# Hybrid decoder step on one core: mLSTM gate rows among the RWKV sample steps, output product evicted by ScalarE, gating ahead of the norm, other piece counts

## The chip, the cores and the metric

One NeuronCore of a Trainium2 chip runs the whole program. The metric is the time of one execution in microseconds (us) on the device. TensorE (PE) multiplies, VectorE (DVE) and ScalarE (ACT) work on elements, SyncE (SP) issues the weight transfers. GpSimd does nothing that matters here.

## The reference, cut to what matters

Two layers, for 256 prompt tokens and 8 sample tokens that share the weights. Only the parts that the change touches are shown.

```python
p = x @ lp['w_in']                                   # D_MODEL 2048 -> 6412 columns
p_rw, p_ret, p_ml = _split(p, [RW_P, RET_P, ML_P])
# RWKV-7: a state per head; the 8 samples take one step from their own state
s = exp(lw_t) * s - (kk_t * a_t) * sa + k_t * v_t    # sa = kk_t . s ; y = r_t . s
o_rw = (groupnorm(y) * g + b + bonus) * gate
# mLSTM: gates of 6 heads, one row of 264 tokens each
ig = CAP * tanh((im + ib) / CAP)
lf = log_sigmoid(CAP * tanh((fm + fb) / CAP))
b = cumsum(lf)                                       # per chunk of 128
m_i = max(running max of (ig - b), m of the chunk before)
s = (q . k) * exp(b_i - b_j + ig_j - m_i);  num = s @ v + ...;  den = sum(s) + ...
hid = num / max(|den|, exp(-m_i))
o_ml = sigmoid(om) * (_rmsnorm_heads(hid) * ml_norm)
# output product, residual, norm, feed-forward
mix = concatenate([o_rw, o_ret, o_ml]) @ lp['w_out']  # 2048 x 2048
x1 = _layernorm(ALPHA * x + mix, ...)
```

## The kernel before

Every large product runs on TensorE in three passes with operands split into a high and a low part. A slab is two blocks of 128 weight rows by 512 columns (512 KB). SP loads it into one of four `w_raw` places, ACT makes `w_hi` (L1202 between the mixers, L1189 in the loops), DVE makes `w_lo` (L1559, L1555), and both have a ring of four places too. So slab s+4 can't be split by ACT before TensorE is through with slab s.

A tile is one weight block of 128x128 for all tokens, that is three matmuls (L672 to L674). A slab holds 8 tiles, two for each of PSUM banks 0 to 3; banks 4 to 7 belong to the mixers. A group is 8 slabs in the input product, and 5 slabs (40 tiles) in the part of the output product that runs among the mLSTM steps. When a group closes, its four banks must be emptied; the next group's first tile in each bank waits on `bank_free` for that (`slab_tiles`, L676). The input groups are emptied by ACT inside `behind` (L1229 for the mLSTM columns), the output groups by DVE in `out_part` (L1574 adds the residual on the way, L1577 adds its low part).

The three mixers are chains of small steps on PE, ACT and DVE. They run one after the other, each beside a stream of tiles: retention beside five input groups, RWKV beside the last six, mLSTM beside 160 tiles of the output product. The steps have names, and a table (`ret_steps`, `rw_last`, `ml_steps`) says how many tiles PE runs ahead of each. `Behind.to(name)` on PE runs tiles up to that count. On ACT and DVE `Parts.to(name)` does the splitting and emptying that belong to those tiles, up to a slab that it works out from the same table, and only then the step's own instructions follow. Each engine has one queue, in the order in which the code is written:

```python
self.goals[name] = max(at_(before), at_(n) - 2, at_(max(n - 1, 0)) // slabs * slabs)
```

By this rule and the table the RWKV step `sa` stands at tile 240 of 368 in layer 0 and at tile 301 in layer 1. Tile 240 is the first of a group, tile 304 is the first of the next. ACT's goal at `sa` is slab 30 (layer 0) and 37 (layer 1), at `sv` it is slab 32 and 40; the emptying of the groups' banks goes with the last slab of a group, 31 and 39. In DVE `then` stands for an instruction, a wait for it, and one more slab's work where the goal of the step that follows leaves room.

The mLSTM part begins with the gate rows: DVE copies two sets of 6 rows (L2138 to L2140), ACT takes tanh, sigmoid and log (L1488 to L1491), DVE scans them and makes maxima (L2146 to L2170), ACT takes exponentials. PE then spreads rows over partitions with 6-row matmuls (`spread_m` L1129, `spread_e` L1138), and the attention steps follow: transposes (L802, L804), scores, numerators (`num0`, `num1`, L827 to L843), sample states (`vt`, `v0` to `v2`, `sy`), and the norm (`sumsq`, `spread` L886, `spread1` L891). The output's last step is the difference `o_lo` (L1867, `a_done`). PE's L1144 and the rest of the output product (`kblock`, L662 to L664) wait for it.

## Time and profile before

| | us |
|---|---|
| median of 3 runs | 2994.88 (2988.88 to 3004.73) |
| profiled execution | 3003.31 |
| its span | 3001.5 |
| PE busy | 2867.8 (96%) |
| PE weight load busy | 2746.3 (91%) |
| DVE busy | 1622.4 (54%) |
| ACT busy | 1171.5 (39%) |

The mean granted TensorE clock of the profiled execution is 0.959 of full speed. TensorE is busy nearly all the time, so its idle time and the stretches at the lower clock are what a reordering can touch. What each wait is for matters more than the busy shares.

### The profile page before, as it was taken

To read this page: it belongs to the slowest core of one execution; us is meant where nothing else is said; L and a number is where in the kernel's file an instruction comes from. 1 tells how busy PE (TensorE), PEld (TensorE's weight loads), DVE (VectorE), ACT (ScalarE), POOL (GpSimd) and SP (SyncE) were. 2 spreads that over 40 slices of the span, in tenths; PEclk is the share of its full clock that TensorE was granted. 3 is DMA by queue.
4 is the path that set the end of the run, shared out by engine and by line. 5 is a ranking of instruction groups with operands and counts; after the bars stand their busy time and mean duration, and the time that the engine had idled before them with its cause. 6 is when DMAs were issued, how large, how long until landed. Compare 5 with 4: busy or idle time off the path is not lost.

```text
span 3001.5 us, 56204 instructions
## 1 busy us (share of the span) xinstructions
PE 2867.8 (96%) x23683; PEld 2746.3 (91%) x23683; DVE 1622.4 (54%) x1696; ACT 1171.5 (39%) x1414; POOL 0.2 (0%) x4
## 2 busy tenths in 40 slices
PE   6999999989999999999999999998899999999995
PEld 5988888869999999999998988887899999999995
DVE  5546546548645455444584565364685454554444
ACT  4335322425533333333363453232463333333333
POOL 0000000000000000000000000000000000000000
PEclk9989999889999999999999999898899999999997
DMA  5624233516555555555564532251455555555451
GB/s 161 191 80 142 86 86 103 153 50 180 188 177 177 179 175 177 179 178 172 180 198 124 154 104 86 64 171 56 133 174 178 177 179 177 176 174 184 164 179 64
DMA packets 278665, 445.03 MB, mean 148 GB/s; under 512 B 45124, under 2 KB 75646, under 8 KB 278182
## 3 DMA queue, kind: packets, MB, share of 16 engines
q1 hardware_dynamic: 276888, 439.29, 46.8%
q10 hardware_dynamic: 1600, 3.12, 0.3%
q8 instruction: 143, 2.34, 0.3%
q14 instruction: 34, 0.28, 0.0%
HBM read 430.58 MB, written 11.78 MB: 147 GB/s over the span
## 4 chain that ended last, share of the span: by engine, by line
PE 88%; DVE 7%; ACT 3%; issue 1%; DMA 1%; SPq 0%; ACTq 0%; DVEq 0%
PE psum L640 18%; PE psum L641 18%; PE psum L639 18%; PE psum L672 6%; PE psum L673 5%; PE psum L674 5%; DVE w_lo L1559 1%; PE psum L869 1%; ACT w_hi L1202 1%; PE psum L662 1%; PE psum L663 1%; PE psum L664 1%; PE psum L1015 1%; PE psum L1030 1%; PE psum L859 1%
## 5 line engine op out<-in xcount | busy, mean ns | idle before, releaser
L1555 DVE TENSOR_TENSOR w_lo<-w_raw,w_hi 128x1024 fp32r<-128x1024 f32 x496 | 606.0, 1225 | 709.2 <-ACT w_hi L1189 707.5
L1189 ACT ACTIVATE w_hi<-w_raw 128x1024 fp32r<-128x1024 f32 x508 | 538.4, 1060 | 933.7 <-PE psum L641 926.9
L639 PE MATMUL psum<-x_hi,w_lo 128*128 128x264 f32 (+3 forms) x3072 | 879.4, 286 | 6.6 <-DVE x_lo L1764 6.6
L641 PE MATMUL psum<-x_hi,w_hi 128*128 128x264 f32 (+3 forms) x3072 | 880.0, 286 | 0.0
L640 PE MATMUL psum<-x_lo,w_hi 128*128 128x264 f32 (+3 forms) x3072 | 879.3, 286 | 0.0
L639 PEld LDWEIGHTS psum<-x_hi,w_lo 128*128 128x128 f32 x3072 | 582.5, 190 | 8.0 <-issue 7.3
L640 PEld LDWEIGHTS psum<-x_lo,w_hi 128*128 128x128 f32 x3072 | 581.9, 189 | 0.2
L641 PEld LDWEIGHTS psum<-x_hi,w_hi 128*128 128x128 f32 x3072 | 580.9, 189 | 0.0
L1559 DVE TENSOR_TENSOR w_lo<-w_raw,w_hi 128x1024 fp32r<-128x1024 f32 x304 | 368.1, 1222 | 262.9 <-ACT w_hi L1202 242.9
L1202 ACT ACTIVATE w_hi<-w_raw 128x1024 fp32r<-128x1024 f32 x292 | 304.1, 1055 | 348.4 <-PE psum L674 268.6
L672 PE MATMUL psum<-x_hi,w_lo 128*128 128x264 f32 (+1 forms) x1376 | 421.5, 306 | 10.4 <-ACT rw_l_below L1453 7.1
L639 PE MATMUL psum<-h_hi,w_lo 128*128 128x264 f32 x1408 | 401.5, 285 | 4.9 <-issue 2.7
L640 PE MATMUL psum<-h_lo,w_hi 128*128 128x264 f32 x1408 | 402.9, 286 | 2.5 <-issue 2.5
L673 PE MATMUL psum<-x_lo,w_hi 128*128 128x264 f32 (+1 forms) x1376 | 405.0, 294 | 0.0
L674 PE MATMUL psum<-x_hi,w_hi 128*128 128x264 f32 (+1 forms) x1376 | 404.4, 294 | 0.0
L641 PE MATMUL psum<-h_hi,w_hi 128*128 128x264 f32 x1408 | 402.0, 286 | 0.0
L672 PEld LDWEIGHTS psum<-x_hi,w_lo 128*128 128x128 f32 x1376 | 270.9, 197 | 31.8 <-issue 17.4
L673 PEld LDWEIGHTS psum<-x_lo,w_hi 128*128 128x128 f32 x1376 | 271.2, 197 | 1.3 <-issue 1.0
L639 PEld LDWEIGHTS psum<-h_hi,w_lo 128*128 128x128 f32 x1408 | 266.6, 189 | 5.4 <-issue 2.9
L674 PEld LDWEIGHTS psum<-x_hi,w_hi 128*128 128x128 f32 x1376 | 270.9, 197 | 0.0
L640 PEld LDWEIGHTS psum<-h_lo,w_hi 128*128 128x128 f32 x1408 | 266.6, 189 | 2.8 <-issue 2.8
L641 PEld LDWEIGHTS psum<-h_hi,w_hi 128*128 128x128 f32 x1408 | 266.4, 189 | 0.0
(433 smaller groups left out, 2691.0 us busy)
## 6 DMA issues: line engine op xcount, KB each, us to landing
w_raw<-in_w_in SPq DMA_DIRECT2D x192, 512.0 KB, 3.6
w_raw<-in_w_gate SPq DMA_DIRECT2D x176, 512.0 KB, 3.5
w_raw<-in_w_up SPq DMA_DIRECT2D x176, 512.0 KB, 3.7
w_raw<-in_w_down SPq DMA_DIRECT2D x176, 512.0 KB, 3.9
w_raw<-in_w_out SPq DMA_DIRECT2D x64, 512.0 KB, 3.8
...
```

Of the source, the lines that this page charges most:

```text
L639: mm(out, w1, bh[:, k, 0:nt], start=(k == 0), stop=False)
L640: mm(out, w0, bl[:, k, 0:nt], start=False, stop=False)
L641: last = mm(out, w0, bh[:, k, 0:nt], start=False, stop=(k == last_k))
L662: mm(out, w1, bh[:, k, 0:nt], start=(k == first), stop=False)
L663: mm(out, w0, bl[:, k, 0:nt], start=False, stop=False)
L672: mm(out, w1, bh[:, k, 0:nt], start=first, stop=False)
L673: mm(out, w0, bl[:, k, 0:nt], start=False, stop=False)
L674: return mm(out, w0, bh[:, k, 0:nt], start=False, stop=last_)
L1189: A(wh[:, j, :, :], raw[:, j, :, :], ACT.Copy).then_inc(S.hi_ready, 1)
L1202: A(wh[:, s % RING, :, :], raw[:, s % RING, :, :], ACT.Copy).then_inc(S.hi_ready, 1)
L1555: TT(wl[:, j, :, :], raw[:, j, :, :], wh[:, j, :, :].bitcast(F32), ALU.subtract).then_inc(S.lo_ready, 1)
L1559: TT(wl[:, s % RING, :, :], raw[:, s % RING, :, :], wh[:, s % RING, :, :].bitcast(F32), ALU.subtract).then_inc(S.lo_ready, 1)
```

## The change

1. **Gate rows.** The mLSTM gate rows are computed in the RWKV part, between its sample and norm steps. DVE's copies and ACT's tanh, sigmoid and log stand behind the second sample instruction of step `sa`; the scans follow in `sv`, `sy` and `gn`; ACT's exponentials stand behind the norm's square root. The rows lie in another place, in what the RWKV part has left. The mLSTM part begins at `spread_m`.
2. **Emptying.** ACT empties the output groups' banks (a plain copy, L1513 of the changed kernel), and DVE adds both residual parts one slab later, as two instructions of 128x1056.
3. **Gating.** ACT applies the output gate's sigmoid and the norm's weights in place ahead of the scores (8 instructions), DVE multiplies the numerators by it ahead of the norm (2 instructions); the two multiplies of 128x1584 behind the norm fall away. The split of the output is made in two parts, 4 heads and 2 heads, and `kblock` waits for the second part only at its fifth block.
4. **Counts.** `ml_steps` has no `rows` step of 70 tiles, and its 70 tiles are spread over the other steps; four RWKV steps get 1 to 3 tiles more.
5. **A wait.** PE's wait for `rw_l_kept` stands behind the 6 tiles of step `x0` and not ahead of them.
6. **Stores.** The waits for the stores of the states are counted on other semaphores, and DVE waits for them later.

```diff
-    rows = at("m_rows", B0 + 27840, [AH, 6, T])
+    rows = at("m_rows", B0 + 6240, [AH, 5, T])
-    rw_last = [('sa', 25), ('sv', 7), ('sy', 16), ('gn', 4), ('gnss', 7), ('gnsp', 8)]
+    rw_last = [('sa', 25), ('sv', 7), ('sy', 19), ('gn', 5), ('gnss', 8), ('gnsp', 9)]
-    ml_steps = [('rows', 70), ('spread_m', 12), ('spread_e', 4), ('turn0', 8), ('turn1', 4), ('score', 4), ('num0', 3),
-                ('num1', 4), ('vt', 9), ('v0', 9), ('v1', 3), ('v2', 3), ('sy', 3), ('sumsq', 5), ('spread', 8), ('spread1', 4)]
+    ml_steps = [('spread_m', 14), ('spread_e', 12), ('turn0', 14), ('turn1', 5), ('score', 5), ('num0', 9), ('num1', 11),
+                ('vt', 13), ('v0', 16), ('v1', 5), ('v2', 5), ('sy', 7), ('sumsq', 13), ('spread', 16), ('spread1', 6)]
...
-                    pe.wait_ge(S.rw_l_kept, 2 * n + 2)
                     for lev in range(5):
                         bg.to(f'x{c}.{lev}')
+                        if lev == 0:
+                            pe.wait_ge(S.rw_l_kept, 2 * n + 2)
...
+                        if i == 4 and g == 0:
+                            pe.wait_ge(S.a_done, 3 * l + 3)
                         kblock(s + i // 2, i % 2, 10 + i, 4 * (g % 2), oh, ol, 10, KB - 1)
...
+                if ml:
+                    A(pml[:, 12:16, 0:T], pml[:, 12:16, 0:T], ACT.Sigmoid)
+                    own(A(ptail[:, 0:2, 0:T], ptail[:, 0:2, 0:T], ACT.Sigmoid))
+                    for h in range(AH):
+                        g = pml[:, 12 + h, 0:T] if h < 4 else ptail[:, h - 4, 0:T]
+                        last = A(g, g, ACT.Identity, scale=col(l, 'ml_norm', h), bias=eps[:, 3:4])
...
-                for name in ('sa', 'sv', 'sy', 'gn', 'gnss'):
+                bg.to('sa')
+                act.wait_ge(S.m_gates_in, l + 1)
+                own(A(rows[:, 0, :], rows[:, 0, :], ACT.Tanh, bias=mlb2[:, 0:1], scale=1.0 / CAP))
+                own(A(rows[:, 1, :], rows[:, 1, :], ACT.Tanh, bias=mlb2[:, 1:2], scale=1.0 / CAP))
+                own(A(rows[:, 1, :], rows[:, 1, :], ACT.Sigmoid, scale=CAP))
+                A(rows[:, 1, :], rows[:, 1, :], ACT.Ln).then_inc(S.m_logf, 1)
+                for name in ('sv', 'sy', 'gn', 'gnss'):
                     bg.to(name)
...
+                def out_one(i):
+                    q = i // 5
+                    for n in range(4 if i % 5 == 4 else 0):
+                        if n < 3:
+                            act.wait_ge(S.bank_done, finished(l, OUT_POS + q, n))
+                        else:
+                            act.wait_ge(S.slab_used, slab0(l, 'out') + i + 1)
+                        A(R1[q][:, n, :], ps[:, n, 0:T], ACT.Copy).then_inc(S.bank_free, 1)
+                    hi1(slab0(l, 'out') + RING + i)
+                bg = Parts(ml_plan, out_one, OUT_POS, OUT_A // 4)
...
-                        STT(R1[q][:, n, :], xh[:, 4 * q + n, 0:T].bitcast(F32), ALPHA, ps[:, n, 0:T],
-                            ALU.mult, ALU.add).then_inc(S.bank_free, 1)
-                    dve.wait_ge(S.bank_free, freed(l, IN_GROUPS + q))
-                    own(STT(R1[q][:, :, :], xl[:, qs_, 0:T].bitcast(F32), ALPHA, R1[q][:, :, :], ALU.mult, ALU.add))
+                if i > 5 and i % 5 == 1 and i < OUT_A + 2:
+                    q = (i - 6) // 5
+                    dve.wait_ge(S.bank_free, freed(l, OUT_POS + q))
+                    for x in (xh, xl):
+                        own(STT(R1[q][:, :, :], x[:, 4 * q:4 * q + 4, 0:T].bitcast(F32), ALPHA, R1[q][:, :, :], ALU.mult, ALU.add))
...
-                    own(TT(ay[:, :, :], ay[:, :, :], over(cols(l, 'ml_norm', AH), T), ALU.mult))
-                    TT(ay[:, :, :], ay[:, :, :], mgate[:, :, :], ALU.mult).then_inc(S.a_out, 1)
+                    TT(ay[:, 4:6, :], ay[:, 4:6, :], ps[:, 4:6, 0:T], ALU.mult).then_inc(S.a_out, 1)
...
-                then(TT(srw[:, :, :, :], srw[:, :, :, :], s1t[:, :, :, :], ALU.subtract))
+                own(TT(srw[:, :, :, :], srw[:, :, :, :], s1t[:, :, :, :], ALU.subtract))
+
+                dve.wait_ge(S.bank_free, freed(l, IN_ORDER.index(TAIL)))
+                dve.wait_ge(S.mlb_loaded, 32 * (l + 1))
+                own(TS(mlb2[:, :], mlb[:, :], 1.0 / CAP, None, ALU.mult))
+                own(v.tensor_copy(rows[:, 0, :], ptail[0:AH, 2, 0:T]))
+                v.tensor_copy(rows[:, 1, :], ptail[32:32 + AH, 2, 0:T]).then_inc(S.m_gates_in, 1)
```

The first place is ACT's queue at step `sa` of layer 0. `w_hi` is the splitting of a slab, `p_ml<-psum` the emptying of a closed group's banks. Before:

```order
L1202 ACTIVATE w_hi<-w_raw 128x1024 [waits slab_used,raw_loaded0]
L1202 ACTIVATE w_hi<-w_raw 128x1024 [waits slab_used,raw_loaded1]
L1202 ACTIVATE w_hi<-w_raw 128x1024 [waits slab_used,raw_loaded2]
L1229 ACTIVATE p_ml<-psum 128x264 [waits bank_done] x3
L1229 ACTIVATE p_ml<-psum 128x264 [waits slab_used]
L1202 ACTIVATE w_hi<-w_raw 128x1024 [waits slab_used,raw_loaded3]
```

Now:

```order
L1203 ACTIVATE w_hi<-w_raw 128x1024 [waits slab_used,raw_loaded0]
L1203 ACTIVATE w_hi<-w_raw 128x1024 [waits slab_used,raw_loaded1]
L1485 ACTIVATE m_rows<-m_rows,ml_bias_scaled 6x264 [waits m_gates_in]
L1486 ACTIVATE m_rows<-m_rows,ml_bias_scaled 6x264 [waits act_steps]
L1487 ACT_TABLE_LOAD
L1487 ACTIVATE m_rows<-m_rows 6x264 [waits act_steps]
L1488 ACT_TABLE_LOAD
L1488 ACTIVATE m_rows<-m_rows 6x264 [waits act_steps]
L1203 ACTIVATE w_hi<-w_raw 128x1024 [waits slab_used,raw_loaded2]
L1230 ACTIVATE p_ml<-psum 128x264 [waits bank_done] x3
L1230 ACTIVATE p_ml<-psum 128x264 [waits slab_used]
L1203 ACTIVATE w_hi<-w_raw 128x1024 [waits slab_used,raw_loaded3]
```

The six gate-row rows, with their wait for DVE's copies, stand ahead of the emptying of the banks; in layer 1 they do too.

The second place is DVE's queue at the same step: `rw_sample` is the sample state, `m_gates_in` is given by the second `m_rows` copy. Before:

```order
L2096 TENSOR_TENSOR rw_sample_t_124<-psum,rw_kk_a 128x2048 [waits rw_sample_sum,dve_steps]
L2098 TENSOR_TENSOR rw_sample<-rw_sample,rw_sample_t_124 128x2048 [waits rw_sample_taken]
L1559 TENSOR_TENSOR w_lo<-w_raw,w_hi 128x1024 [waits hi_ready,dve_steps]
L1559 TENSOR_TENSOR w_lo<-w_raw,w_hi 128x1024 [waits hi_ready]
L2101 TENSOR_TENSOR rw_sample_t_124<-psum,p_rw 128x2048 [waits rw_sample_sum]
L2102 TENSOR_TENSOR rw_sample<-rw_sample,rw_sample_t_124 128x2048 [waits dve_steps]
```

Now:

```order
L2115 TENSOR_TENSOR rw_sample_t_124<-psum,rw_kk_a 128x2048 [waits rw_sample_sum,dve_steps]
L2117 TENSOR_TENSOR rw_sample<-rw_sample,rw_sample_t_124 128x2048 [waits rw_sample_taken]
L2121 TENSOR_SCALAR ml_bias_scaled<-ml_bias 6x2 [waits mlb_loaded,bank_free,dve_steps]
L2122 COPY m_rows<-p_tail 6x264 [waits dve_steps]
L2123 COPY m_rows<-p_tail 6x264 [waits dve_steps]
L1578 TENSOR_TENSOR w_lo<-w_raw,w_hi 128x1024 [waits hi_ready] x2
L2126 TENSOR_TENSOR rw_sample_t_124<-psum,p_rw 128x2048 [waits rw_sample_sum]
L1578 TENSOR_TENSOR w_lo<-w_raw,w_hi 128x1024 [waits hi_ready,dve_steps]
L2127 TENSOR_TENSOR rw_sample<-rw_sample,rw_sample_t_124 128x2048
```

The three small gate-row instructions stand behind the second `rw_sample` instruction and ahead of the two `w_lo`, which wait for `w_hi` rows that ACT now has behind its gate rows.

The third place is DVE's queue at the mLSTM steps `num0` and `num1` of layer 0, where PE waits for `a_y` and then for `a_kv_sample`. Before:

```order
L1795 COPY a_state<-psum 128x384 [waits a_summed]
L1559 TENSOR_TENSOR w_lo<-w_raw,w_hi 128x1024 [waits hi_ready,dve_steps]
L1801 COPY a_y<-psum 128x6x128
L1799 SCALAR_TENSOR_TENSOR a_state<-a_state,m_cdecay,psum 128x128 [waits a_summed]
L1799 SCALAR_TENSOR_TENSOR a_state<-a_state,m_cdecay,psum 128x128 [waits dve_steps] x2
L1801 COPY a_y<-psum 128x6x128 [waits dve_steps]
L1809 TENSOR_TENSOR a_kv_sample<-sum_selectors,a_kw 128x144 [waits a_sample_loaded,a_y_kept]
```

Now:

```order
L1807 COPY a_state<-psum 128x384 [waits a_summed]
L1589 SCALAR_TENSOR_TENSOR resid_0_83<-x_hi,resid_0_83 128x1056 [waits bank_free,dve_steps]
L1589 SCALAR_TENSOR_TENSOR resid_0_83<-x_lo,resid_0_83 128x1056 [waits dve_steps]
L1578 TENSOR_TENSOR w_lo<-w_raw,w_hi 128x1024 [waits hi_ready,dve_steps]
L1813 COPY a_y<-psum 128x6x128
L1811 SCALAR_TENSOR_TENSOR a_state<-a_state,m_cdecay,psum 128x128 [waits a_summed]
L1578 TENSOR_TENSOR w_lo<-w_raw,w_hi 128x1024 [waits hi_ready,dve_steps]
L1811 SCALAR_TENSOR_TENSOR a_state<-a_state,m_cdecay,psum 128x128
L1578 TENSOR_TENSOR w_lo<-w_raw,w_hi 128x1024 [waits hi_ready,dve_steps]
L1811 SCALAR_TENSOR_TENSOR a_state<-a_state,m_cdecay,psum 128x128
L1578 TENSOR_TENSOR w_lo<-w_raw,w_hi 128x1024 [waits hi_ready,dve_steps]
L1813 COPY a_y<-psum 128x6x128
```

The residual's two instructions stand between `a_state` and the first `a_y`, and three `w_lo` stand between the `a_state` rows ahead of the second `a_y`; the last of them needs a slab that PE reaches only 10 tiles into the fill of `vt`.

## Rows read from the trace of the kernel before

**Rows 1.** The page, busy time, share of the span and instructions:

```profile
PE 2867.8 (96%) x23683; PEld 2746.3 (91%) x23683; DVE 1622.4 (54%) x1696; ACT 1171.5 (39%) x1414; POOL 0.2 (0%) x4
```

**Rows 2.** Waits of PE, whole span: in total, times, longest:

```profile
PE psum L672 <- DVE resid L1574: 13.2, 5, 4.7
...
PE psum L1144 <- DVE o_lo L1867: 8.8, 2, 5.1
...
PE psum L672 <- ACT rw_l_below L1453: 7.1, 4, 1.8
PE psum L1129 <- DVE m_rows L2161: 6.7, 2, 3.3
...
PE psum L662 <- DVE resid L1574: 4.2, 2, 2.1
...
PE psum L886 <- DVE ln_sum L1850: 2.4, 2, 1.2
```

**Rows 3.** Stretches with the busy time of PE, PEld, DVE, ACT, POOL; PEclk:

```profile
520.00:530.00 10.00, 10.00 (x85) 10.00 (x84) 4.78 (x4) 3.25 (x4) 0.00 (x0) 1.00 1.02 274
571.00:591.00 20.00, 20.00 (x67) 17.02 (x68) 7.56 (x17) 4.66 (x15) 0.00 (x0) 0.50 0.08 27
1977.00:1980.50 3.50, 3.50 (x23) 2.98 (x22) 1.01 (x1) 0.00 (x0) 0.00 (x0) 1.00 0.28 65
1981.00:1984.00 3.00, 3.00 (x15) 3.00 (x15) 2.93 (x6) 0.00 (x0) 0.00 (x0) 0.50 0.00 0
```

**Rows 4.** Timeline of PE at step `sa`, layer 0: start, us, instruction:

```profile
469.53 3.60 PE L1089 MATMUL psum<-rw_sample_t,base_tables 128*128 128x512 f32 x8
472.56 0.69 PE L672 MATMUL psum<-x_hi,w_lo 128*128 128x264 f32 x1
```

**Rows 5.** Timeline of ACT and DVE at `sa`, layer 0:

```profile
467.82 0.84 ACT L1229 ACTIVATE p_ml<-psum 128x264 f32<-128x264 f32 x2
...
476.13 2.29 DVE L2098 TENSOR_TENSOR rw_sample<-rw_sample,rw_sample_t 128x2048 f32<-128x2048 f32 x1
```

**Rows 6.** Timeline of DVE and ACT at the gate rows, layer 0:

```profile
539.62 0.29 DVE L2140 COPY m_rows<-p_tail 6x264 f32<-6x264 f32 x1
...
539.94 0.52 ACT L1488 ACTIVATE m_rows<-m_rows,ml_bias_scaled 6x264 f32<-6x264 f32 x1 [0.70 <-DVE m_rows L2140]
...
542.75 1.28 ACT L1491 ACT_TABLE_LOAD   x1
544.05 0.42 ACT L1491 ACTIVATE m_rows<-m_rows 6x264 f32<-6x264 f32 x1
```

**Rows 7.** Timeline of PE, DVE at `sa`, layer 1:

```profile
1947.35 0.69 PE L672 MATMUL psum<-x_hi,w_lo 128*128 128x264 f32 x1
...
1950.35 2.29 DVE L2098 TENSOR_TENSOR rw_sample<-rw_sample,rw_sample_t 128x2048 f32<-128x2048 f32 x1
```

**Rows 8.** The page and groups by line: x count, busy us, mean ns, idle before:

```profile
L1202 ACT ACTIVATE w_hi<-w_raw 128x1024 fp32r<-128x1024 f32 x292 | 304.1, 1055 | 348.4 <-PE psum L674 268.6
...
L1559 DVE TENSOR_TENSOR w_lo<-w_raw,w_hi 128x1024 fp32r<-128x1024 f32 x304 | 368.1, 1222 | 262.9 <-ACT w_hi L1202 242.9
...
L1577 DVE SCALAR_TENSOR_TENSOR resid<-x_lo,resid 128x1056 f32<-128x1056 f32 x8 | 10.1, 1258 | 0.3
```

**Rows 9.** Timeline of ACT behind the first turned heads, layer 0:

```profile
593.16 0.49 ACT L1330 ACTIVATE a_ktok<-psum 128x384 f32<-128x384 f32 x1 [11.37 <-PE psum L804]
...
594.03 0.39 ACT L1332 ACTIVATE a_vtok<-psum 128x256 f32<-128x256 f32 x1
```

**Rows 10.** Wait of PE between 603 and 612 us:

```profile
PE psum L827 <- DVE a_y L1801: 1.2, 1, 1.2
```

**Rows 11.** Timeline of DVE between `num1` and `vt`, layer 0:

```profile
616.87 0.96 DVE L1801 COPY a_y<-psum 128x768 f32<-128x768 f32 x1 [0.15 <-DVE a_state L1799]
...
618.20 0.19 DVE L1812 COPY a_kv_sample<-p_ml 128x48 f32<-128x48 f32 x1
```

**Rows 12.** Timeline of DVE behind the first `rw_l` copies, layer 0:

```profile
335.01 0.76 DVE L2041 TENSOR_TENSOR rw_lmask<-rw_l,masks 128x256 f32<-128x256 f32 x2 [1.04 <-ACT rw_l L1451]
```

More of the change, by code:

```diff
@@ L925, in _ @@
                 bg.to('in')
-                pe.wait_ge(S.a_done, 2 * l + 1)
+                pe.wait_ge(S.a_done, 3 * l + 1)
                 pe.wait_ge(S.rw_in, l + 1)
@@ L1479, in _ @@
                   scale=1.0 / RW_HD).then_inc(S.rw_gn_std, 1)
+                act.wait_ge(S.m_rows_x, l + 1)
+                A(rows[:, 1, :], rows[:, 1, :], ACT.Exp)
+                A(rows[:, 4, :], rows[:, 4, :], ACT.Exp)
+                A(men[:, :], rows[:, 2, :], ACT.Exp, scale=-1.0).then_inc(S.m_rows_e, 1)
                 bg.to('gnsp')
@@ L1843, in attention @@
                     TT(mdn[:, :], mdn[:, :], men[:, :], ALU.max).then_inc(S.m_guarded, 1)
+                    dve.wait_ge(S.a_y_ready, n + 1)
+                    dve.wait_ge(S.a_squares, n + 1)
+                    dve.wait_ge(S.a_gate, n + 1)
+                    TT(ay[:, 0:4, :], ay[:, 0:4, :], pml[:, 12:16, 0:T], ALU.mult)
+                    own(TT(ay[:, 4:6, :], ay[:, 4:6, :], ptail[:, 0:2, 0:T], ALU.mult))
                     dve.wait_ge(S.m_eps, l + 1)
@@ L2104, in _ @@
                 then(TT(bonus[:, :, :], bonus[:, :, :], over(cols(l, 'rw_lnx_b', 4), T), ALU.add))
+                dve.wait_ge(S.m_logf, l + 1)
+                for c in range(NCH):
+                    cs = slice(CH * c, CH * c + CH)
+                    then(v.tensor_tensor_scan(rows[:, 2, cs], ones[0:AH, :], rows[:, 1, cs], 0.0, ALU.mult, ALU.add))
+                then(v.tensor_copy(rows[:, 2, SEQ:T], rows[:, 1, SEQ:T]))
+                STT(rows[:, 0, :], rows[:, 0, :], CAP, rows[:, 2, :], ALU.mult, ALU.subtract).then_inc(S.m_rows_c, 1)
                 bg.to('sy')
@@ L2112, in _ @@
                 last.then_inc(S.rw_gn_in, 1)
+                dve.wait_ge(S.m_rows_c, l + 1)
+                dve.wait_ge(S.m_m_loaded, 16 * (l + 1))
+                then(v.memset(rows[:, 4, 0:CH], 0.0))
+                then(v.tensor_copy(rows[:, 4, SEQ:T], mst[:, :]))
+                for c in range(NCH):
+                    cs = slice(CH * c, CH * c + CH)
+                    then(v.tensor_tensor_scan(rows[:, 3, cs], rows[:, 0, cs], rows[:, 0, cs], mcol[:, :] if c else 0.0, ALU.max, ALU.max))
+                    if c + 1 < NCH:
+                        then(TT(mcol[:, :], rows[:, 2, CH * c + CH - 1:CH * c + CH], rows[:, 3, CH * c + CH - 1:CH * c + CH], ALU.add))
+                        then(v.tensor_copy(rows[:, 4, CH * c + CH:CH * c + 2 * CH], mcol[:, :].to_broadcast([AH, CH])))
+                TT(rows[:, 3, SEQ:T], rows[:, 0, SEQ:T], rows[:, 4, SEQ:T], ALU.max).then_inc(S.m_rows_m, 1)
                 bg.to('gn')
@@ L2116, in _ @@
                 STT(yt[:, :, :], ps[:, 4:8, 0:T], -1.0 / RW_HD, yt[:, :, :], ALU.mult, ALU.add).then_inc(S.rw_gn_c, 1)
+                dve.wait_ge(S.m_rows_m, l + 1)
+                then(TT(rows[:, 2, :], rows[:, 2, :], rows[:, 3, :], ALU.add))
+                then(v.tensor_copy(mfin[:, 0:NS], rows[:, 2, SEQ:T]))
+                then(v.tensor_copy(mfin[:, NS:NS + 1], rows[:, 2, SEQ - 1:SEQ]))
+                for c in range(NCH):
+                    cs = slice(CH * c, CH * c + CH)
+                    then(TS(rows[:, 1, cs], rows[:, 0, cs], rows[:, 3, CH * c + CH - 1:CH * c + CH], None, ALU.subtract))
+                then(TT(rows[:, 1, SEQ:T], rows[:, 0, SEQ:T], rows[:, 3, SEQ:T], ALU.subtract))
+                TT(rows[:, 4, :], rows[:, 4, :], rows[:, 3, :], ALU.subtract).then_inc(S.m_rows_x, 1)
                 bg.to('gnss')
@@ L2144, in _ @@
-                for c in range(NCH):
-                    cs = slice(CH * c, CH * c + CH)
-                    own(v.tensor_tensor_scan(rows[:, 2, cs], ones[0:AH, :], rows[:, 1, cs], 0.0, ALU.mult, ALU.add))
-                own(v.tensor_copy(rows[:, 2, SEQ:T], rows[:, 1, SEQ:T]))
-                STT(rows[:, 0, :], rows[:, 0, :], CAP, rows[:, 2, :], ALU.mult, ALU.subtract).then_inc(S.m_rows_c, 1)
-                bg.to('rows')
-                dve.wait_ge(S.m_rows_c, l + 1)
-                dve.wait_ge(S.m_m_loaded, 16 * (l + 1))
@@ L2153, in _ @@
-                then(v.memset(rows[:, 4, 0:CH], 0.0))
-                then(v.tensor_copy(rows[:, 4, SEQ:T], mst[:, :]))
-                for c in range(NCH):
-                    cs = slice(CH * c, CH * c + CH)
-                    then(v.tensor_tensor_scan(rows[:, 3, cs], rows[:, 0, cs], rows[:, 0, cs], mcol[:, :] if c else 0.0, ALU.max, ALU.max))
-                    if c + 1 < NCH:
-                        then(TT(mcol[:, :], rows[:, 2, CH * c + CH - 1:CH * c + CH], rows[:, 3, CH * c + CH - 1:CH * c + CH], ALU.add))
-                        then(v.tensor_copy(rows[:, 4, CH * c + CH:CH * c + 2 * CH], mcol[:, :].to_broadcast([AH, CH])))
@@ L2161, in _ @@
-                TT(rows[:, 3, SEQ:T], rows[:, 0, SEQ:T], rows[:, 4, SEQ:T], ALU.max).then_inc(S.m_rows_m, 1)
-                dve.wait_ge(S.m_rows_m, l + 1)
-                then(TT(rows[:, 2, :], rows[:, 2, :], rows[:, 3, :], ALU.add))
-                then(v.tensor_copy(mfin[:, 0:NS], rows[:, 2, SEQ:T]))
-                then(v.tensor_copy(mfin[:, NS:NS + 1], rows[:, 2, SEQ - 1:SEQ]))
-                for c in range(NCH):
-                    cs = slice(CH * c, CH * c + CH)
-                    then(TS(rows[:, 1, cs], rows[:, 0, cs], rows[:, 3, CH * c + CH - 1:CH * c + CH], None, ALU.subtract))
@@ L2169, in _ @@
-                then(TT(rows[:, 1, SEQ:T], rows[:, 0, SEQ:T], rows[:, 3, SEQ:T], ALU.subtract))
-                TT(rows[:, 4, :], rows[:, 4, :], rows[:, 3, :], ALU.subtract).then_inc(S.m_rows_x, 1)
                 bg.to('spread_m')
```

91 lines of the change are left out of this document (36 added, 55 removed).

## Prediction

> **What bounds the kernel now.** I read the page first: TensorE is busy for 2867.8 of 3001.5 us [rows 1], so DVE and ACT matter only where PE waits for them. Then PE's waits. Among those that the change touches, the longest are those of a tile for a bank that DVE has yet to empty (13.2 us), of L1144 for the output's last difference (8.8), of a tile behind the RWKV pairs for ACT's copies (7.1), of the first 6-row spread for the gate rows (6.7), of the later output product for the last banks (4.2), of the second spread for a reciprocal (2.4) [rows 2]. Together 42.4 us, 1.4% of the span. That is the most that can be won in waits. Then the stretches. A tile is three matmuls: 85 matmuls in 10 us at the full clock are 0.36 us a tile, 15 in 3 us at half are 0.6 [rows 3]. Behind the gate rows PE is busy for all of 20 us and gets half the clock [rows 3]; that costs up to 10 us a layer and is in no list of waits. Last, both queues were followed in the timeline around the places to which instructions go.
>
> **The waits that go.** Without the `rows` step the first spread finds its rows long finished: 6.7 us go, if the RWKV part makes them in time. ACT empties the banks: the waits for `resid` go in their old form, 13.2 and 4.2. The end of the mLSTM part loses two multiplies of 128x1584, so the 8.8 go as well, and the second spread now has 16 tiles (5.8 us) ahead of it and not 8: 2.4 go. The wait for `rw_l_kept`: 7.1 us in four times, 1.8 each [rows 2]. It would be paid behind 6 tiles, 2.2 us, which covers 1.8. The masks that the next matmuls want are done at 335.77 [rows 12], some 2.0 us behind the last pair matmul (my estimate from the copies' wait of 1.8), still inside 2.2. So 7.1 go whole; were the masks later, what is left is below 0.3 a time.
>
> **The waits that come, mLSTM part.** Each layer has three.
> (a) In `turn0` to `turn1` the first output group closes at tile 40, which is where `turn0` stands. ACT's goals put the emptying behind that step's copies (1.26 us from 593.16 to 594.42 [rows 9]) and one `w_hi` (1.06 [rows 8]), then 0.4 for a bank (0.84 for two [rows 5]): 2.7 and about 0.2 until ACT starts, 2.9 us in which PE can't open the next group. Before, this closing lay in the `rows` fill.
> (b) At `num1` DVE has two residual instructions more, 1.26 each [rows 8], in a chain that was 4 tiles and a wait of 1.2 long [rows 10], 2.6 us: 5.1 now, against 11 tiles or 4.0. About 1.2 is waited as before. No gain, no loss.
> (c) Ahead of `vt` the last of three `w_lo` needs a slab for which PE must reach tile 80, ten tiles into a fill that starts at 70: 3.6 us, an emptying 0.4, `w_hi` 1.06, `w_lo` 1.22 [rows 8], then the copies from 616.87 to 618.39, 1.5 [rows 11]: 7.8. PE's 13 tiles take 4.7. Wait 3.1.
> (d) The end: from the second spread DVE has a multiply like the residual's in size (1.26), two residual instructions (2.5), two `w_lo` (2.4), a half-size multiply (0.7, estimate from the same row), the first difference (1.26): 8.1. PE has 15 tiles and a small step, 6.4. Wait 1.7; then the last group's emptying stands behind ACT's half-size copy, a `w_hi` and four banks, 1.4 more. 3.1 in all, against 6.5 a layer before (8.8 and 4.2 over two).
> Together 9.1 a layer, 18.2. The other fills are longer than what stands behind them: `v0` has 16 tiles, 5.8 us, where three sample multiplies and one more take 4.9.
>
> **The wait that comes, RWKV part.** This is the term that decides. In layer 0 `sa` stands at the first tile of a group. The banks of the closed group are emptied in ACT's part for `sv`. In the trace that happened early, from 467.82 [rows 5], and PE went from L1089 straight into the fill at 472.56 [rows 4]. Now the gate rows stand ahead of it in ACT's queue, and they wait for DVE's copies behind the second sample instruction. That instruction ends at 478.42 [rows 5]; three small ones of at most 0.29 with gaps take 0.8 [rows 6]: 479.2. ACT's chain with two table loads took from 539.94 to 544.47, 4.5 [rows 6]: 483.8. A `w_hi` 1.06 and the first bank 0.4: 485.3. PE, which began this fill at 472.56, stalls for 12.7 us. In layer 1 three tiles can still run, to 1948.7; DVE ends at 1952.64 [rows 7] and with 0.8 at 1953.4; the listing has one table load (1.28 [rows 6]) fewer, 3.3: 1956.7; two `w_hi` and a bank, 2.5: 1959.2. Stall 10.5. Together 23.2 us. DVE's two `w_lo` behind its copies wait for the same ACT rows, so the third sample instruction is late too, but PE must first run its 7 tiles and L1089, and 19 tiles then cover it. The added scans, copies and maxima of DVE (under 3 us in each of `sy` and `gn`, estimate from the 0.29 of a 6-row copy) lie beside fills of 5 and 8 tiles with their matmuls; at most 0.5 us is seen.
>
> The Trainium skill bears on this ("TensorE: Matmul & The Clock Gate", the section on the array of sub-arrays, the lines on engine queue depths): ScalarE and VectorE take their queues strictly in order, only TensorE's can pull weight loads forward. If ACT could pass its waiting gate row, the stall would be nothing and the sum 23 us better; by that rule it is as worked out. No row here shows ACT overtaking.
>
> **The clock.** In 571 to 591 about 10 us a layer are lost at half clock. Now 14 tiles stand ahead of the first 6-row step, 12 between the two and 14 behind. Bounds: nothing back, or all 10. I take half, since the fills are dense and the steps between them unchanged: 10 us over two layers. Against it, after an idle of 12.7 or 10.5 us the clock will be low: 7 tiles at 0.6 and not 0.36 are 1.7, L1089's four matmuls (3.6 us [rows 4]) up to 3.6 more; bounds 0 and 5.3, I take 2.5 a layer, 5. Waits (a) and (c) are each about as long as the one for `resid` that they follow (3 against up to 4.7), so their clock is left as it was.
>
> The same page of the Trainium skill (the sections on HAM oscillation and on what matters for a kernel) holds that idle gaps between bursts lower the clock. By that alone all 20 us would come back, since the idle of 3.3 ahead of the spread goes, and the sum would be 10 us better. But between 1977.0 and 1980.5 PE was busy for all 3.5 us, a part of it with 8-row matmuls, and from 1981 the clock was at half [rows 3]. So the trace doesn't agree, and small matmuls alone can lower it.
>
> **Sum.** Waits that go 42.4; that come 18.2 and 23.2: gain 1.0. Clock: 10 less 5, gain 5. Small waits under 1.3 us that the longer fills cover, of the kind of rows 10 (scores, samples; no rows shown): about 3. Gain 9 us. The profiled execution took 3003.31, so 2994 by it; the median shown is 2994.88, so 8.4 lower, and I apply the gain to the median: 2986 us, 0.3% below. A run of this kernel can't tell less than 0.5%, 15 us, from no change.
>
> **Rivals.**
> *No stall.* ACT's goals are met early enough, or PE's fill doesn't need those banks. For it: DVE's copies could come sooner. Against: the listing, and DVE is busy without a gap up to 478.4. Gain 9 and 23 and 5: 2958. Chance 0.12.
> *The clock comes back whole* (the page's rule, as a mechanism: the 6-row steps alone don't lower it in so dense a stretch). Gain 9 and 10 more and some 3 at the end: 2973. Chance 0.19.
> *The low clock behind the stall lasts.* PE comes cold out of 12.7 us and meets 512-column matmuls, then the 64x1 sample matmuls and the norm's small ones. If the clock is low for the 7 tiles, L1089, the 19 tiles (4.6) and the norm steps (3), each layer pays 13 and not 2.5; with the half that I count back in the spreads missing too (10), the kernel is 22 us slower: 3017. It decides from 24 us more than in my sum for "slower by over 0.5%". Chance 0.15.
> *My forecast*, 2973 to 3000: 0.54.
>
> The range 2965 to 3006 leaves out the first rival and about half of the third. Faster by over 0.5% (below 2979.9): 0.12 of the first, 0.14 of the second and 0.12 of my own, 0.38. Within: 0.40 of my own, 0.05 of the second and 0.02 of the third, 0.47. Slower: 0.13 of the third and 0.02 of my own, 0.15.
>
> **What would show it.** Right: a wait of PE's tile for an emptying (`p_ml`) of 12 to 13 us near 472 and of 10 to 11 near 1948; no wait for `rw_l_below`; one of about 3 behind `turn0`, another ahead of L850, and less than 2 ahead of L1144; part of the 20 us behind the first spread at full clock. Wrong: no idle at `sa`; or waits of 3 us elsewhere in the mLSTM part; or a low clock through all of the sample steps.

## The result

| kernel | median of its runs, us | lowest to highest | before, same chips | ratio | 95% interval |
|---|---|---|---|---|---|
| changed | 2979.80 (13 runs) | 2972.89 to 2987.13 | 3001.46 (13 runs) | 0.9937 | 0.9915 to 0.9959 |

The changed kernel is 0.6% faster: 19 us by the ratio, with an interval from 12 to 26 (3001.46 times 0.0041 and 0.0085). The forecast was 2986, the range 2965 to 3006. The profiled execution took 2977.48 us, span 2975.7, mean granted clock 0.963 of full speed (0.959 before).

The page of the changed kernel, which answers to [rows 1]:

```profile
PE 2846.6 (96%) x23683; PEld 2732.7 (92%) x23683; DVE 1615.9 (54%) x1674; ACT 1179.8 (40%) x1455; POOL 0.2 (0%) x4
```

PE executes the same 23683 matmuls in 21.2 us less busy time. Its idle time, span less busy, went from 133.7 to 129.1 us. So four fifths of what this execution gained is not in any wait: the same matmuls ran faster. Some 5 us of that are not the change's doing. Up to the 1200th matmul, ahead of everything that it moves, PE was busy for 169.7 us before and for 164.5 now:

```profile
0.00:198.20 198.20, 169.70 (x1201) 152.94 (x1201) 104.10 (x109) 77.07 (x93) 0.20 (x4) 0.97 0.51 155
```

```profile
0.00:193.10 193.10, 164.50 (x1199) 148.57 (x1200) 104.02 (x109) 77.08 (x93) 0.20 (x4) 0.98 0.52 159
```

The kernels of the experiments, which do not differ there either, stand on these two levels alike: 164.6 us in the kernel before with one wait moved (experiment 2), 169.3 in a kernel made from the changed one (experiment 11). The ratio of the medians, 19 us, is the measure of the gain, and not the 25.8 of these two executions.

Waits of PE in the changed kernel, whole span (in total, times, longest, in us), against [rows 2]. Line numbers on PE are one lower than before:

```profile
PE psum L671 <- ACT p_ml L1230: 16.3, 4, 12.1
...
PE psum L671 <- DVE w_lo L1578: 10.8, 2, 10.0
...
PE psum L849 <- DVE a_kv_sample L1824: 6.2, 2, 3.1
...
PE psum L671 <- ACT resid L1513: 5.3, 2, 2.7
PE psum L826 <- DVE a_y L1813: 4.2, 4, 1.3
...
PE psum L858 <- DVE m_sample L1839: 3.0, 2, 1.5
...
PE psum L661 <- ACT resid L1513: 1.6, 2, 1.3
...
PE psum L1143 <- DVE o_lo L1877: 1.1, 1, 1.1
```

Gone are the waits for `rw_l_below` (7.1) and `m_rows` (6.7), the 13.2 for DVE's `resid` and the reciprocal's 2.4. New are the two of 12.1 and 10.0 us, the `a_kv_sample` and the `m_sample`. The chain at the 12.1, PE's timeline at step `sa` of layer 0 (the bracket is the idle ahead and what ended it), beside [rows 4]:

```profile
473.56 0.56 PE L671 MATMUL psum<-x_hi,w_lo 128*128 128x264 f32 x1 [12.05 <-ACT p_ml L1230]
...
477.88 3.60 PE L1089 MATMUL psum<-rw_sample_t,base_tables 128*128 128x512 f32 x8
```

and ACT's timeline of the same place, beside [rows 5]:

```profile
467.68 0.51 ACT L1485 ACTIVATE m_rows<-m_rows,ml_bias_scaled 6x264 f32<-6x264 f32 x1 [14.36 <-DVE m_rows L2123]
...
471.78 0.42 ACT L1488 ACTIVATE m_rows<-m_rows 6x264 f32<-6x264 f32 x1
472.11 1.04 ACT L1203 ACTIVATE w_hi<-w_raw 128x1024 fp32r<-128x1024 f32 x1
473.06 1.18 ACT L1230 ACTIVATE p_ml<-psum 128x264 f32<-128x264 f32 x4
```

ACT stands idle for 14.36 us in front of its first gate row, then takes 4.5 us for the rows, makes one `w_hi`, and only then frees the bank that PE has wanted since 461.5. Nothing on ACT or DVE was short of time; the order in one queue did it. In layer 1 the same idle of 10.0 is put down to `w_lo`, since DVE's splitting follows ACT's.

Now the clock. Stretches of the changed kernel (busy time of the engines; the third number from the right is PEclk), beside the 20 us at 0.50 in [rows 3]:

```profile
548.50:551.50 3.00, 3.00 (x15) 2.36 (x16) 0.00 (x1) 0.00 (x0) 0.00 (x0) 1.00 0.72 183
552.00:555.50 3.50, 3.50 (x20) 3.50 (x19) 2.59 (x2) 0.88 (x3) 0.00 (x0) 0.56 0.36 111
555.50:562.00 6.50, 6.50 (x43) 5.97 (x43) 0.43 (x1) 4.64 (x12) 0.00 (x0) 0.97 0.15 23
562.00:567.00 5.00, 5.00 (x31) 5.00 (x30) 4.83 (x8) 0.00 (x0) 0.00 (x0) 0.66 0.39 108
```

The first spread runs at the full 2.4 GHz, and behind it the clock falls to 1.2 GHz only for some 3 us at a time (the two rows with 0.56 and 0.66 are means over such a piece and its neighbourhood at full clock). The second spread's matmuls by form (count, busy us, mean ns):

```profile
L1137 PE MATMUL psum<-m_rows,selectors 6*128 6x256 f32 x24 | 7.9, 418 | 0.0
```

In the trace of before the same group is 14.4 us at a mean of 701 ns, that of the first spread went from 10.8 (634 ns) to 5.7 (381 ns), and the 6x8 ones that alternate with the second's from 5.2 to 3.3: 13.5 us in all.

### The profile page after: what moved, and what is told of

It reads as the page before. It is cut to its first block, busy times and chain, and to the rows that moved or that the text cites. A ratio compares the mean times of both kernels' runs of the same rounds, so it can differ in the third digit from the quotient of the medians.

```text
span 2975.7 us, 56241 instructions
## 1 busy us (share of the span) xinstructions
PE 2846.6 (96%) x23683; PEld 2732.7 (92%) x23683; DVE 1615.9 (54%) x1674; ACT 1179.8 (40%) x1455; POOL 0.2 (0%) x4
## 4 chain that ended last, share of the span: by engine, by line
PE 89%; DVE 6%; ACT 3%; issue 2%; DMA 0%; ACTq 0%; DVEq 0%
PE psum L639 19%; PE psum L640 19%; PE psum L638 19%; PE psum L671 7%; PE psum L672 6%; PE psum L673 6%; DVE w_lo L1578 1%; ACT w_hi L1203 1%; PE psum L868 1%; PE psum L661 1%; PE psum L662 1%; PE psum L663 1%; PE psum L1015 1%; PE psum L1030 1%; PE psum L826 1%
```

## The experiments

Each was timed beside runs of the kernel before on the same chip; the ratios are to that kernel, and differences between kernels are taken from the ratios (0.001 is 3 us). Each ratio is known to about 0.002, so a difference between two kernels is uncertain by some 7 to 11 us; rows of the traces are from one execution each. None leaves out a part of the computation; the four with GpSimd add writes to a buffer that nobody reads.

**1. The gate rows one place further back in ACT's queue.**

```diff
                 bg.to('sa')
+                bg.to('sv')
                 act.wait_ge(S.m_gates_in, l + 1)
                 own(A(rows[:, 0, :], ..., ACT.Tanh, ...))
...
-                for name in ('sv', 'sy', 'gn', 'gnss'):
+                for name in ('sy', 'gn', 'gnss'):
```

> The changed kernel, with ScalarE's tanh, sigmoid and log of the gate rows moved behind its part for step sv (so the splitting and the emptying of the closed group's banks stand ahead of them). Theory: the two idles of PE at step sa, 12.1 us in layer 0 and 10.0 us in layer 1, are this order in ScalarE's queue and nothing else. They go, and PE waits for no p_ml above 3 us; the time falls by 22 to 27 us against the changed kernel's 2980, to about 2955, ratio to the kernel before 0.985. Rival one, the stall only moves: ScalarE's rows are later, DVE's scans too, and PE waits as long in steps sy, gn or at the first spread; ratio 0.993. Rival two, the cold clock behind the stall costs as much again (7 tiles, the 512-column and the 64x1 matmuls): then 35 us are won, ratio 0.981.

Measured: 2957.65 us, ratio 0.985 (0.9821 to 0.9879). PE's waits and then ACT's timeline in this kernel:

```profile
PE psum L671 <- ACT p_ml L1230: 4.2, 3, 2.6
...
PE psum L1099 <- DVE rw_sample L2128: 1.9, 2, 1.5
```

```profile
467.46 0.51 ACT L1486 ACTIVATE m_rows<-m_rows,ml_bias_scaled 6x264 f32<-6x264 f32 x1 [8.22 <-DVE m_rows L2124]
```

Both long idles are gone. ACT still sits idle ahead of its rows, but nobody stands behind it. PE idles 109.4 us and not 129.1 (19.7 less) and is busy for 2842.4 and not 2846.6 (4.2 less). Of these 4.2, 2.0 lie around the stall of layer 1 and none around that of layer 0, where the kernel without the stall has 10 us at half clock from 477 us on as well; 1.7 lie ahead of layer 1's stall, where the two kernels do the same (527 matmuls took 78.3 us busy and then 76.6). The timing says 0.0087, 26 us, the trace 22 of stalls and 2 of clock. Neither rival holds: a wait for `rw_sample` of 1.9 is all that came.

**2. and 3. The wait for `rw_l_kept`, alone and undone.** Into the kernel before, and out of the changed one:

```diff
-                    pe.wait_ge(S.rw_l_kept, 2 * n + 2)
                     for lev in range(5):
                         bg.to(f'x{c}.{lev}')
+                        if lev == 0:
+                            pe.wait_ge(S.rw_l_kept, 2 * n + 2)
```

> The kernel before, with only PE's wait for the kept pair blocks (rw_l_kept) moved behind the 6 tiles of step x0. Theory: the 7.1 us for rw_l_below go whole, and some 2 us of half clock behind them come back: 9 us less than the kernel before, ratio 0.997. Rival one: the wait goes over to the masks or to the next matmul of x0, so nothing changes: ratio 0.9995. Rival two, that this one line brings most of the whole change (its four gaps let the clock fall more often than I count): ratio 0.994.

> The changed kernel with PE's wait for rw_l_kept put back ahead of the 6 tiles of step x0. The one line alone brought 12 us in the kernel before, where my sum had 7.1. Theory: the parts add, the 7.1 us of waits for rw_l_below come back and with them about 4 us of half clock behind them: 2991, ratio to the kernel before 0.997. Rival: in the changed kernel the line is worth only its waits, 7 us: 2987, ratio 0.995. Second rival: it is worth nothing there, since the stall at sa stands behind it: 2980, ratio 0.993.

Measured: alone 2990.86 us, 0.9961 (0.9944 to 0.9977), which is 12 us (7 to 17); undone 2991.46 us, 0.9972 (0.9956 to 0.9987), 0.0035 or 10.5 us above the changed kernel. The two agree with each other and with the theory; by the times alone the 7.1 us of waits would do as well. What decides is the trace. Two stretches behind such a wait, with it (changed kernel, wait put back), and then the same matmuls in the changed kernel, without it:

```profile
401.00:404.00 3.00, 3.00 (x20) 2.76 (x21) 1.71 (x2) 0.02 (x1) 0.00 (x0) 0.50 0.08 10
1875.50:1878.50 3.00, 3.00 (x33) 2.76 (x31) 0.25 (x2) 0.11 (x1) 0.00 (x0) 0.50 0.00 0
```

```profile
391.60:393.25 1.65, 1.65 (x21) 1.51 (x21) 1.30 (x3) 1.62 (x3) 0.00 (x0) 1.00 0.12 41
1861.40:1863.00 1.60, 1.60 (x33) 1.45 (x32) 1.56 (x4) 0.30 (x2) 0.00 (x0) 1.00 0.05 10
```

PE is busy all the time in each, and the waits were 1.8 us at most. Yet behind them these 20 and 33 matmuls take 3 us, and 1.65 and 1.6 without them: each such stretch costs some 1.4 us. It does not come every time. Of the four waits two are followed by one here (behind the other two, at 336 and 1811 us, the clock is at 1.00), and three in the kernel before (336, 401 and 1875 us). So by the traces the line is worth 7.1 and 3 to 4 us more, which is what both times say.

**4. Gate rows and table back, the rest kept.** The rows are computed at the head of the mLSTM part again, `ml_steps` is that of the kernel before.

```diff
-    ml_steps = [('spread_m', 14), ('spread_e', 12), ('turn0', 14), ...
+    ml_steps = [('rows', 70), ('spread_m', 12), ('spread_e', 4), ('turn0', 8), ...
```

> The changed kernel with the gate rows put back into the mLSTM part and the mLSTM table of the kernel before (rows 70 and so on). ScalarE's emptying, the early gating and the moved wait stay. Theory: the waits for resid (17.4 us) and for the last difference (8.8 to about 2) and for rw_l_below (7.1) go, no stall at sa comes (so 22 us better there than the changed kernel), but the first spread waits for its rows as before (6.7) and the spreads run at half clock (12 us). Sum against the kernel before: 17 + 7 + 7 less new waits for ScalarE's emptying of 3 to 5 us, about 27 us less, 2975, ratio 0.991: as fast as the changed kernel or faster, so that the moved rows and the new table bring nothing by themselves. Rival one: the emptying's waits only change their name, and ratio is 0.995 or more, so that the moved rows are what won. Rival two: the clock follows the longer idles saved and gives 10 us more, ratio 0.988.

Measured: 2986.68 us, 0.9947 (0.9929 to 0.9966); nearer to rival one. Its waits of PE:

```profile
PE psum L826 <- DVE a_scores L1804: 15.1, 4, 7.5
...
PE psum L885 <- DVE ln_sum L1869: 7.7, 2, 3.8
...
PE psum L1130 <- DVE m_rows L2180: 5.7, 2, 2.9
...
PE psum L671 <- ACT resid L1505: 3.8, 3, 1.5
```

The theory had 27 us, 16 came. DVE's wait for `resid` of 13.2 did fall to 3.8, but 15.1 us for the scores and 7.7 for the norm came. With the old small fills (4 and 5 tiles) DVE's two residual instructions, its multiply of the gates and ACT's eight gating instructions stand in the way. Without the moved wait's 12 us, emptying and early gating gave about 4, no more than the noise. With the new table and the gate rows moved and well placed (experiment 1) there are 0.0097 or 29 us more. The two were not tried apart, so how much of it is the table's is open; the 22.8 us of waits for the scores and the norm are 0.5 in the changed kernel, with its larger fills.

**5. Late gating.** ACT's sigmoids and DVE's two multiplies of 128x1584 stand behind the norm again.

```diff
-                    TT(ay[:, 4:6, :], ay[:, 4:6, :], ps[:, 4:6, 0:T], ALU.mult).then_inc(S.a_out, 1)
+                    own(TT(ay[:, 4:6, :], ay[:, 4:6, :], ps[:, 4:6, 0:T], ALU.mult))
+                    own(TT(ay[:, :, :], ay[:, :, :], over(cols(l, 'ml_norm', AH), T), ALU.mult))
+                    TT(ay[:, :, :], ay[:, :, :], mgate[:, :, :], ALU.mult).then_inc(S.a_out, 1)
```

> The changed kernel with the gating of the kernel before: ScalarE's sigmoids late into a buffer of their own, and VectorE's two multiplies of 128x1584 behind the norm. Theory: the two multiplies (some 1.9 us each, from the 1.26 of 128x1056) stand on the path from the second spread to the last difference, and 15 tiles no longer cover it: PE waits 3 to 4 us more a layer ahead of L1143 or of its next block, with 1 to 2 us of half clock behind: 2988 to 2990, ratio 0.996. Rival: the freed instructions ahead of the norm (two multiplies, eight of ScalarE) give back as much in the waits for a_y and for the copies ahead of vt, and the time is the changed kernel's, 0.993.

Measured: 2989.15 us, 0.9952 (0.9937 to 0.9968), 0.0015 or 4.5 us above the changed kernel; the two intervals overlap. The trace is clearer:

```profile
PE psum L1144 <- DVE o_lo L1874: 7.4, 2, 6.0
```

1.1 became 7.4, and `a_y` and `a_kv_sample` wait as long as in the changed kernel (4.2 and 6.2), so nothing is given back. The theory had 3 to 4 us a layer; the 6.3 in all are 4.9 in layer 0 and 1.4 in layer 1.

**6. The spreads close together.** 22 and 4 tiles ahead of the spreads, not 14 and 12.

```diff
-    ml_steps = [('spread_m', 14), ('spread_e', 12), ('turn0', 14), ...
+    ml_steps = [('spread_m', 22), ('spread_e', 4), ('turn0', 14), ...
```

> The changed kernel, with 22 and 4 tiles ahead of the two 6-row spreads in place of 14 and 12 (the sum is the same, and the fill behind them too). No idle stands ahead of the first spread in either. Theory: the spreads' 6x256 matmuls got the full clock back (L1128 and L1137 from 25.2 to 13.6 us in all) because more tiles lie between the two; with 4 between them they fall back to some 23 us and the tiles between and behind to half clock: 8 to 14 us slower than the changed kernel, ratio to the kernel before 0.997. Rival: they got it back because the idle of 3.3 us ahead of the first spread is gone; then this kernel is as fast as the changed one, ratio 0.993, and both spreads stay below 15 us.

Measured: 2984.26 us, 0.9945 (0.9922 to 0.9968), 0.0008 above the changed kernel. By form, the second spread here:

```profile
L1137 PE MATMUL psum<-m_rows,selectors 6*128 6x256 f32 x24 | 9.7, 495 | 1.9 <-DVE a_scores L2194 1.9
```

495 ns is a quarter of the way from 418 back to 701, and the first spread stayed at 5.7 us. My theory (tiles between the spreads) explains 2 of 13.5 us. The time lies in reach of both the theory and its rival; the durations decide. The theory fell, and a new one was formed: the idle ahead of the first spread, 3.3 us in each layer before [rows 2].

**7. to 10. An idle put in by hand.** GpSimd, idle otherwise, writes small memsets when PE has used up a slab, and PE waits for the last. In three of the four kernels 16 and 10 tiles stand ahead of the two spreads, in `idle_and_close` 24 and 4. `idle_in_fill` has the wait 6 tiles behind the second spread. The cut shows `idle_ahead`; the two with the long idle write 92 memsets and not 48.

```diff
+        @block.gpsimd
+        def _(pool):
+            for l in range(DEPTH):
+                pool.wait_ge(S.slab_used, slab0(l, 'out') + 2)
+                for k in range(48):
+                    last = nc.gpsimd.memset(idle[:, ...], 0.0)
+                last.then_inc(S.start_loaded, 1)
...
                 bg.to('spread_m')
                 pe.wait_ge(S.m_rows_x, l + 1)
+                pe.wait_ge(S.start_loaded, 48 + l + 1)
```

> The changed kernel with an idle of PE put in by hand directly ahead of the first 6-row spread of each layer: behind 16 tiles PE waits for 48 small memsets of the else idle GpSimd, some 3 us (10 tiles between the two spreads, so that the sum stays). The kernel before had such an idle there (6.7 us in two) and then 20 us at half clock. Theory, formed on the run with the spreads close together: the idle is what took the clock, not the small number of tiles between the spreads. Then the 6x256 matmuls go from 0.38 and 0.42 us back to 0.55 or more, and the kernel is slower than the changed one by the idles (6) and 10 us or more: 2996 or above, ratio to the kernel before 0.998 to 1.000. Rival: the 16 tiles ahead and 10 between keep the clock up whatever stands ahead; only the idles are paid, 2986, ratio 0.995.

> As idle_ahead (PE idle by hand ahead of the first 6-row spread, 16 tiles ahead and 10 between the spreads), but with 92 memsets in place of 48: the 48 made an idle of 1.85 us a layer and cost nothing that shows, and the kernel before had 3.3. Theory A: the length of the idle decides. With 3.3 us the clock is at half from the first spread on and for some 20 us, as in the kernel before; the 6x256 matmuls go to 0.6 us and more, and the kernel is slower than the changed one by 6.6 of idle and 15 to 20 of clock: 3003, ratio to the kernel before 1.000. Theory B: the idle costs only itself where 16 and 10 tiles stand around the spread: 2987, ratio 0.9955.

> The same idle of some 3.3 us ahead of the first spread, and the spreads close together as in the kernel before (24 tiles ahead, 4 between, 12 behind). Theory A, the length of the idle decides: half clock for some 20 us, as in idle_ahead_long, ratio 1.000. Theory B, it takes both, idle and closeness: this kernel alone of the four (idle or not, close or not) has the 20 us at half clock; 3003 here against 2987 in idle_ahead_long. If neither of the two shows it, something else that went with the gate rows kept the clock down in the kernel before, and it stays open.

> The same idle by GpSimd's 48 memsets, but 6 tiles behind the second spread, in the middle of a fill of plain tiles (tile 32). Theory: an idle among wide matmuls costs little more than itself, 6 us and up to 3 of clock: 2986 to 2989, ratio 0.995 to 0.996, and the spreads stay at 0.38 and 0.42 us. Rival: any idle of 3 us costs 8 us of half clock a layer, wherever it stands: 3000, as much as the idle ahead of the spread.

The column of the half clock gives the time at 1.2 GHz in the 45 us from 5 us ahead of the first spread, both layers together. The kernel before has 41 us there, and its 6x256 took 634 and 701 ns.

| kernel | idle, both layers, us | tiles between | 6x256 of the spreads, mean ns | half clock, us | median us | ratio | interval |
|---|---|---|---|---|---|---|---|
| changed | 0 | 12 | 381, 418 | 17 | 2979.80 | 0.9937 | 0.9915 to 0.9959 |
| spreads_close | 0 and 1.9 | 4 | 382, 495 | 24 | 2984.26 | 0.9945 | 0.9922 to 0.9968 |
| idle_ahead | 3.7 | 10 | 448, 417 | 24 | 2983.70 | 0.9934 | 0.9911 to 0.9956 |
| idle_ahead_long | 6.6 | 10 | 565, 543 | 38 | 2995.54 | 0.9971 | 0.9955 to 0.9987 |
| idle_and_close | 6.6 | 4 | 621, 577 | 41 | 2998.96 | 0.9987 | 0.9968 to 1.0006 |
| idle_in_fill | 3.5 | 10 | 381, 470 | 24 | 2991.61 | 0.9955 | 0.9940 to 0.9971 |

The stretch behind the idle in idle_ahead_long, and then in idle_and_close:

```profile
549.50:559.50 10.00, 10.00 (x35) 8.40 (x36) 4.20 (x4) 1.27 (x5) 0.00 (x0) 0.50 0.16 47
563.50:570.00 6.50, 6.50 (x26) 6.00 (x26) 3.18 (x6) 0.00 (x0) 0.00 (x0) 0.50 0.01 3
```

```profile
562.00:582.00 20.00, 19.75 (x67) 16.75 (x67) 8.28 (x13) 3.62 (x12) 0.00 (x0) 0.50 0.20 53
```

The idle of 3.3 us brings the half clock back: 38 us of it with 10 tiles between the spreads, 41 with 4, against 17 and 24 without an idle. So theory B of `idle_ahead_long`, that the idle costs only itself, fell by its trace; theory A had the clock right, but its time (1.000) did not come either. What closeness adds to it is small: in `idle_and_close` the half clock of layer 0 is one piece of 20 us as in [rows 3] (in layer 1 two, 10 and 7 us), in `idle_ahead_long` it comes in pieces of 10 us and less. The theory that it takes both, idle and closeness, holds for the single piece of 20 us alone. An idle of 1.85 us a layer costs nothing that can be measured, within some 9 us, and its theory (2996 or above) fell; one of 3.3 us costs 0.0034, 10 us, of which 6.6 are itself; the same idle with the spreads close costs 0.0050, 15 us. In the middle of a fill two idles of 1.75 us cost 0.0018, 5 us with the 3.5 of their own, as its theory had it. The steps between neighbouring rows of the table lie inside the intervals (0.9971 and 0.9987 above all); the means of the spreads and the stretches carry the order. They scatter too: in `idle_in_fill` the second spread stands ahead of the idle, and took 470 and not 418, and the kernel of experiment 11, with 14 and 12 tiles like the changed one, has 7 us at half clock there and not 17. So 17 and 24 are not told apart by one execution; 17 and 38 are.

**11. Other counts.** Experiment 1 with two groups closing where ACT can empty them at once.

```diff
-    ... ('turn0', 14), ('turn1', 5), ('score', 5), ... ('vt', 13), ('v0', 16), ('v1', 5), ('v2', 5), ...
+    ... ('turn0', 16), ('turn1', 4), ('score', 4), ... ('vt', 10), ('v0', 17), ('v1', 6), ('v2', 6), ...
```

> rows_behind_sv with other counts: turn0 16, turn1 4, score 4 (the first output group now closes two tiles ahead of turn0, so that ScalarE's emptying stands ahead of its copies), and vt 10, v0 17, v1 6, v2 6 (the third group closes where vt stands, so that the copies for vt wait for no emptying; more tiles ahead of v2). Theory: the wait for resid of 2.7 a layer behind turn0 falls to about 1, the 3.1 ahead of L849 goes and a wait of 1.8 for resid behind vt comes, the 1.5 for m_sample goes: 4 us a layer, 8 in all, 2950, ratio to the kernel before 0.982. Rival: the waits only change their places (the copies of turn0 come later, v0's fill opens later) and the time stays at 2957.65, ratio 0.985.

Measured: 2942.16 us, 0.9804 (0.9780 to 0.9828), the fastest of all: 59 us ahead of the kernel before and 14 ahead of experiment 1 by the ratios, where 8 were expected; the two intervals touch, so it may be 8. Its waits of PE:

```profile
PE psum L671 <- ACT resid L1514: 3.8, 2, 1.9
...
PE psum L858 <- DVE m_sample L1840: 1.6, 2, 0.8
...
PE psum L849 <- DVE a_kv_sample L1825: 0.4, 2, 0.2
```

Against experiment 1 these three groups lose 8.7 us (5.3, 3.0 and 6.2 there), but waits elsewhere (1.6 more for a `w_lo`, 1.6 more for `rw_tmp`, 1.0 more each for the last `resid` and `o_lo`) take 4.9 back on balance: PE's whole idle is 105.6 and not 109.4, 3.8 less. Busy time fell by 12.1 (2842.4 to 2830.3), at the same matmuls. Once more the clock gave more than the waits in this execution; of that 5 us (half of 17 less 7) lie around the spreads, whose fills were not changed, so part of it is scatter.

Not tried: DVE's emptying with the new table. The third boundary, tile 120, lies inside the fill of `sumsq`, and DVE waits for `a_sumsq` ahead of that fill's work, so that PE and DVE would wait for each other. By this reading, which no run tests, ACT's emptying is a condition of the new table. What it is worth by itself is open.

## Why the prediction was right, and where its sum was off

The direction is that of the sum, and 2979.80 us lies in the range; the gain is 19 us by the ratio where the sum had 9. The side of 0.5% is not the one that had the largest chance (within, 0.47): 2979.80 lies just below the bound of 2979.9, on the side that had 0.38, and the interval of the ratio, 0.41 to 0.85%, leaves both open. That the forecast of 2986 came within 6 us is in part luck. It was taken from a median before of 2994.88 over 3 runs; over 13 runs it is 3001.46, and the same gain from there would be 2992. Term by term:

- **The stall at `sa`.** Forecast 12.7 and 10.5, in the trace 12.05 and 10.04, and experiment 1 gives it back: 0.0087, 26 us. Of cold clock behind it 5 was counted; the traces show 2. The mechanism was right to 1 us. "No stall" is refuted.
- **The waits that go and come in the mLSTM part.** (a) 2.9 forecast, 2.7; (b) 1.2, 1.3; (c) 3.1, 3.1; (d) 3.1 a layer, in the trace 2.4 in layer 0 and 0.4 in layer 1. Missed: 1.5 a layer for `m_sample` ahead of `v2`, which I had called covered by longer fills, and waits for `p_ml` of 2.6 at 518 and 1.5 at 1986, where the kernel before had 0.6 in all. The gate rows are not their cause: with the rows back in the mLSTM part (experiment 4) they are there too, 4.2 in all. The changed counts of the RWKV steps are a likely one, which was not tried. PE's idle in all fell by 4.6, forecast 1.0 and about 3.
- **The wait for `rw_l_kept`.** I counted its 7.1 and no clock. It measured 12 alone and 10.5 undone, and the traces have 7.1 and 3 to 4 us of half clock. This is the first term that was mis-sized, by 3 to 5 us: what I counted at the stall (half clock behind a pause) comes behind two or three of these four pauses of 1.8 us too, and the stretches behind them in the trace of before show it: 3.2 us at 0.50 from 335.7 on.
- **The clock at the spreads.** "I take half", 10 us over two layers. The spreads' own matmuls gave 13.5, with the tiles among them more. This is the second mis-sized term. The step that failed is the reading of 1977.0 to 1981 [rows 3]: that the clock can fall with no idle ahead is true (552 to 555.5 above is such a case), but such a piece is 3 us long and costs some 1.5, not 10. The 20 us at half clock came from the idle of 3.3 ahead of the spread, as the kernels with that idle (38 and 41 us) and without (17 and 24) show.
- **The rival "the clock comes back whole"** had 2973 and the mechanism that turned out nearer. The Trainium skill ("TensorE: Matmul & The Clock Gate", the section on what matters for a kernel) warns of idle gaps between bursts. The runs agree in part: 3.3 us ahead of the spread costs 3 to 8 us beyond itself by the ratios, and 1.8 us ahead of the RWKV levels left a stretch at half clock in two or three cases of four. But 1.85 us ahead of the spread cost nothing that can be measured, and from 552 us on the clock fell with no gap at all.
- **"The low clock behind the stall lasts"** is refuted: in layer 0 tiles were back at full clock at 477.4 us, 3.8 us behind the stall's end, and L1089 took the same 3.60 us as before.

Of the 21.2 us that the busy time fell, the spreads are 13.5, the stretches behind the moved wait some 4, and 5 is the scatter ahead of the first change; the stall costs 2 the other way. That leaves nothing larger than the scatter between runs of one kernel (13 runs spread over 14 us). Open is why the same matmuls, in kernels that do not differ there, run now at one and now at the other clock.
